# Four more projection units of the two layers as products of split operands, ahead of the gates

## What is computed

```
h    = rms_norm(x, attn_norm_g)
proj = h @ w_in                       # 1024 x 4768, float32
c_q, c_kv, k_rope, gq, gk, gv, pool_in, gate_logits = split_columns(proj, IN_SIZES)
o_mla, o_gqa, o_pool = mla_branch(...), gqa_branch(gq, gk, gv), pool_branch(pool_in)
gates  = sigmoid(gate_logits)         # 3 x 1024 columns
merged = sum over branches of gates[b] * (o_b @ w_branch_b)
x = x + merged @ w_out
x = x + (silu(u_gate) * u_val) @ w_down,   u = conv(rms_norm(x) @ w_up)
```

## Time and profile before

| what | us |
|---|---|
| median of 3 runs | 2156.4 (2155.51 to 2159.56) |
| the profiled execution | 2156.41 |
| its span, first to last instruction | 2154.6 |
| outside the span | 1.8 |
| TensorE busy in the span | 2047.8 (95%) |
| VectorE busy | 893.4 (41%) |
| ScalarE busy | 628.6 (29%) |
| layer 0: from 1220 us on; layer 1: from 1687 us on | about 467 each |

### The profile page before, as it was taken

How to read it: one execution, slowest core, us unless ns; L and a number is a source line. 1 busy time by engine, 2 the same in 40 slices (tenths; PEclk the granted TensorE clock), 3 DMA queues, 4 the chain that set the end, 5 groups by cost and what they waited for, 6 DMA issues and landing times.

```text
span 2154.6 us, 31774 instructions
## 1 busy us (share of the span) xinstructions
PE 2047.8 (95%) x12318; PEld 1314.1 (61%) x12319; DVE 893.4 (41%) x1608; ACT 628.6 (29%) x967; POOL 31.1 (1%) x45
## 2 busy tenths in 40 slices
PE   6998999999999999999999999999999999999999
PEld 4863333333333333333333598879999888789999
DVE  2522221112212221122122346866885348766874
ACT  1422111111111111111111225443654144634553
POOL 0000000000000000000000020000000020000000
PEclk9998999999999999999999999999999999999999
DMA  9786999399999999999499564413654554334563
GB/s 345 268 328 265 393 417 402 134 417 417 417 419 418 417 417 418 419 418 417 179 371 417 217 195 128 147 55 103 203 189 158 140 158 132 111 99 145 171 204 108
DMA packets 222040, 580.36 MB, mean 269 GB/s; under 512 B 23520, under 2 KB 142048, under 8 KB 185984
## 3 DMA queue, kind: packets, MB, share of 16 engines
q1 hardware_dynamic: 221952, 579.09, 70.7%
HBM read 577.74 MB, written 1.31 MB: 269 GB/s over the span
## 4 chain that ended last, share of the span: by engine, by line
PE 69%; DMA 11%; SPq 8%; DVE 6%; ACT 3%; issue 3%; ACTq 0%; DVEq 0%
PE bank L1080 13%; DMA ring<-in_w_gu 9%; PE bank L1136 8%; PE bank L807 6%; SPq L680 4%; SPq L682 4%; PE bank L1424 3%; PE bank L1425 3%; PE bank L1426 3%; PE bank L1032 3%; PE bank L1046 3%; PE bank L1211 2%; PE bank L877 2%; PE bank L1213 2%; PE bank L1212 2%
## 5 line engine op out<-in xcount | busy, mean ns | idle before, releaser
L1080 PE MATMUL bank<-ring,heap 128*64 128x512 f32 x2176 | 494.6, 603 | 30.4 <-DMA ring<-in_w_gu 30.4
L1080 PEld LDWEIGHTS bank<-ring,heap 128*64 128x64 f32 x2176 | 149.0, 138 | 359.2 <-issue 266.0
L2045 DVE TENSOR_SCALAR heap<-bank 128x256 f32<-128x256 f32 (+1 forms) x72 | 26.7, 412 | 725.2 <-PE bank L1080 696.5
L1136 PE MATMUL bank<-ring,heap 128*64 128x512 f32 (+1 forms) x1152 | 255.1, 595 | 0.0
L1424 PE MATMUL bank<-h_hi,w_hi 128*128 128x256 f32 x640 | 181.7, 284 | 3.4 <-DVE w_lo L2321 3.4
L2321 DVE TENSOR_TENSOR w_lo<-ring,w_hi 128x2048 fp32r<-128x2048 f32 (+1 forms) x64 | 142.4, 2226 | 97.6 <-ACT w_hi L1739 97.6
L1425 PE MATMUL bank<-h_lo,w_hi 128*128 128x256 f32 x640 | 181.1, 283 | 0.0
L1426 PE MATMUL bank<-h_hi,w_lo 128*128 128x256 f32 x640 | 181.1, 283 | 0.0
L1575 ACT ACT_TABLE_LOAD x32 | 41.1, 1283 | 471.8 <-DVE heap L2045 470.2
L1136 PEld LDWEIGHTS bank<-ring,heap 128*64 128x64 f32 (+1 forms) x1152 | 78.7, 135 | 150.7 <-issue 145.0
L1739 ACT ACTIVATE w_hi<-ring 128x2048 fp32r<-128x2048 f32 (+1 forms) x64 | 119.1, 1860 | 145.4 <-PE bank L1426 85.9
(11 more groups left out here) (336 smaller groups left out, 3065.3 us busy)
## 6 DMA issues: line engine op xcount, KB each, us to landing
ring<-in_w_gu SPq DMA_DIRECT2D x256, 1024.0 KB, 19.1
ring<-in_w_down SPq DMA_DIRECT2D x128, 1024.0 KB, 21.4
ring<-in_ffn_w_up SPq DMA_DIRECT2D x44, 1024.0 KB, 7.7
ring<-in_w_in SPq DMA_DIRECT2D x32, 1024.0 KB, 5.6
ring<-in_w_ada SPq DMA_DIRECT2D x24, 1024.0 KB, 10.8
ring<-in_ffn_w_down SPq DMA_DIRECT2D x16, 1024.0 KB, 6.7
ring<-in_w_out SPq DMA_DIRECT2D x8, 1024.0 KB, 4.9
ring<-in_w_in SPq DMA_DIRECT2D x3, 2048.0 KB, 27.1
```

Of the source, the lines that this page charges most:

```text
L1080: last = mm(psum[g][both[f], :], xgT[:, k % 4, k // 4, :], wt[:, g, :, :, f, :].rearrange("p i c n -> p (i c) n"), start=False, stop=k == ...
L1136: last = mm(psum[2][FEW * f:FEW * f + n, :], hidT[:, o:o + n], wt[:, 512 * f:512 * (f + 1)], start=k == 0, stop=k == DT - 1)
```

## The change

In each layer four of the plain units become split units: `gq1`, `po0`, `gk`, `po1`. `cq`, `ckv`, the key part, `gq0` and `gv` stay plain.

- The order on PE after `ckv`: `gq0` plain, `gq1` split, `po0` split, `gv` plain, `gk` split, `po1` split, then the small sums and the gates as before. `gq1` and `gk` are now products of `h`, so DVE only copies them out of PSUM.
- The list of pieces has `w_po0` ahead of `w_gkv`. With that `w_po0` is early; `w_po1` waits for `gq0` and `ckv`, `ga0` for the split of `w_gq1`, `ga1` for that of `w_po0`, and the later pieces lie one place further in the ring.
- ACT makes `w_hi` of `gq1` and `po0` right after its first root of the layer, ahead of `var1`; DVE makes the two `w_lo` ahead of its work on `ss1`.
- `h_hi` and `h_lo` are made in halves, right after `h`; the scaling of `xT` comes behind them. The first split unit waits for the first half, and at k = 4 for the second.
- `w_hi` of `gk` is made by ACT behind `gq1`, of `po1` behind `po0`, of `ga0` behind `gk`, of `ga1` behind `po1`; DVE follows each.

```diff
-NG, NB, NW = 12, 6, 22
+NI, NG, NB, NW = 4, 16, 6, 26
+FIRST = ("w_gq1", "w_po0", "w_gkv", "w_po1")
...
-        layer = [("w_lat", 8 * 416), ("w_gq0", 8 * 256), ("w_gq1", 8 * 256), ("w_gkv", 8 * 384), ("w_po0", 8 * 256),
+        layer = [("w_lat", 8 * 416), ("w_gq0", 8 * 256), ("w_gq1", 8 * 256), ("w_po0", 8 * 256),
+                 ("w_gkv", 8 * 384), ("w_po1", 8 * 256), ("ga0", 8 * 256), ...
...
+                        if first and k % 4 == 0:
+                            done("h1", 2 + k // 4)
...
+                def by_unit(name, n):
+                    done("wlo", n + 1)
+                    b = halves(lay(name))
+                    for a in range(2):
+                        last = split_tile(b[:, a, :], early_unit(n)[2:], P * a, (h_hi, h_lo), DT, n == 0 and a == 0)
+                    last.then_inc(lay_full.sem, 1)
...
-                for i in range(2):
-                    arrived(f"w_gq{i}")
-                    tiles(f"gq{i}", piece(lay_stream, f"w_gq{i}", 8), 0, raw)
+                arrived("w_gq0")
+                tiles("gq0", piece(lay_stream, "w_gq0", 8), 0, raw)
+                by_unit("gq1", 0)
+                by_unit("po0", 1)
                 arrived("w_gkv")
-                tiles("gk", w, 0, raw)
                 ... gv ...
-                for i in range(2):
-                    arrived(f"w_po{i}")
-                    tiles(f"po{i}", piece(lay_stream, f"w_po{i}", 8), 0, h)
+                by_unit("gk", 2)
+                by_unit("po1", 3)
...                                                     (ACT)
                 f(L["rs"][:, 1, :], c2, ACT.Sqrt).then_inc(S["std1"].sem, 1)
+                lead(0)
+                lead(1)
                 ready("var1")
...
-                f(h_hi[:, :, :], L["h"], ACT.Copy).then_inc(S["hhi"].sem, 1)
+                for i in range(2):
+                    f(h_hi[:, 4 * i:4 * i + 4, :], L["h"][:, 4 * i:4 * i + 4, :], ACT.Copy).then_inc(S["hhi"].sem, 1)
+                full("gq1")
+                lead(2)
+                out_of("po0", L["pool"][:, 0:2, PAD:PAD + T])
+                lead(3)
+                out_of("gv", L["gv"], lambda b: two(b)[:, :, 0:P])
+                full("gk")
+                lead(4)
                 out_dve("gk")
...
-                out_of("gv", L["gv"], lambda b: two(b)[:, :, 0:P])
-                lead(0)
-                out_of("po0", L["pool"][:, 0:2, PAD:PAD + T])
                 out_of("po1", L["pool"][:, 2:4, PAD:PAD + T])
-                lead(1)
+                lead(5)
...                                                     (DVE)
                 ready("vecs")
+                rest_early(0)
+                rest_early(1)
                 r1 = L["rs"][:, 0, :]
...
+                ready("h1")
+                for i in range(2):
+                    ready("hhi", i + 1)
+                    v.tensor_tensor(h_lo[:, 4 * i:4 * i + 4, :], ...).then_inc(S["h1"].sem, 1)
                 c.mark(v.tensor_tensor(xT[:, :, :], xT[:, :, :], ...))
                 taken(by_token(L["gq"][:, 0:2, :], two(full("gq0"))))
-                taken(by_token(L["gq"][:, 2:4, :], two(full("gq1"))))
-                taken(by_token(L["gk"], two(full("gk"))))
+                taken(v.tensor_copy(L["gq"][:, 2:4, :], two(full("gq1"))))
+                rest_early(2)
+                rest_early(3)
+                taken(v.tensor_copy(L["gk"], two(full("gk"))))
                 own("gk")
                 c.settle()
-                ready("hhi", 1)
-                v.tensor_tensor(h_lo[:, :, :], ...).then_inc(S["h1"].sem, 1)
-                rest_early(0)
+                rest_early(4)
                 b = two(full("sslat"))
```

More of the change, by code:

```diff
@@ L324, in build @@
         exp_stream = Stream(EXPERT, RING)
-        layer = [("w_lat", 8 * 416), ("w_gq0", 8 * 256), ("w_gq1", 8 * 256), ("w_gkv", 8 * 384), ("w_po0", 8 * 256),
-                 ("w_po1", 8 * 256), ("ga0", 8 * 256), ("ga1", 8 * 256), ("w_uq", 2 * 768), ("w_ukv", 1024), ("ga2", 8 * 256),
-                 ("pool_w", 4 * P)] + [(f"ga{n}", 8 * 256) for n in range(3, NG)] \
+        layer = [("w_lat", 8 * 416), ("w_gq0", 8 * 256), ("w_gq1", 8 * 256), ("w_po0", 8 * 256),
+                 ("w_gkv", 8 * 384), ("w_po1", 8 * 256), ("ga0", 8 * 256), ("ga1", 8 * 256), ("w_uq", 2 * 768), ("w_ukv", 1024), ("ga2", 8 * 256),
+                 ("pool_w", 4 * P)] + [(f"ga{n}", 8 * 256) for n in range(3, NG - NI)] \
             + [(f"br{b}{h}", 4 * 512) for h in range(2) for b in range(3)] + [(f"wo{i}", 8 * 256) for i in range(4)] \
@@ L332, in build @@
         lay_stream = Stream(layer, LRING, again=True)
-        LAY_LAST = {"w_lat": "ckv", "w_gq0": "gq0", "w_gq1": "gq1", "w_gkv": "gv", "w_po0": "po0", "w_po1": "po1",
+        LAY_LAST = {"w_lat": "ckv", "w_gq0": "gq0", "w_gkv": "gk",
                     "w_uq": "uq3", "w_ukv": "uv1", "pool_w": "pl1", "up0": "up1"}
@@ L502, in build @@
         heads = [f"m{h}" for h in range(NH)] + [f"g{h}" for h in range(NH)]
-        order = [("ss1", "dve"), ("cq", "dve"), ("ckv", "dve"), ("gq0", "dve"), ("gq1", "dve"), ("gk", "dve"),
-                 ("gv", "act"), ("po0", "act"), ("po1", "act"), ("sslat", "dve"), ("ssgq", "dve"),
+        order = [("ss1", "dve"), ("cq", "dve"), ("ckv", "dve"), ("gq0", "dve"), ("gq1", "dve"), ("po0", "act"),
+                 ("gv", "act"), ("gk", "dve"), ("po1", "act"), ("sslat", "dve"), ("ssgq", "dve"),
                  ("ssgk", "dve"), ("ga0", "act"), ("ga1", "act")]
@@ L534, in build @@
         S = {name: signal(f"l_{name}", per) for name, per in {
-            "vecs": 1, "sq1": 4, "var1": 1, "std1": 2, "xg": 2 * DT, "h1": 6, "lsq": 1, "lvar": 1, "lstd": 1, "lat": 1,
+            "vecs": 1, "sq1": 4, "var1": 1, "std1": 2, "xg": 2 * DT, "h1": 7, "lsq": 1, "lvar": 1, "lstd": 1, "lat": 1,
             "gsq": 1, "gvar": 1, "gstd": 1, "gn": 1, "rope_g": 1, "qvar": 1, "qstd": 1,
@@ L565, in early_unit @@
         def early_unit(n):
-            name, rows = (f"ga{n}", DT) if n < NG else (f"br{(n - NG) % 3}{(n - NG) // 3}", 4) if n < NG + NB else \
+            name, rows = (FIRST[n], DT) if n < NI else (f"ga{n - NI}", DT) if n < NG else (f"br{(n - NG) % 3}{(n - NG) // 3}", 4) if n < NG + NB else \
                 (f"wo{n - NG - NB}", DT)
             hi, lo = (x[:, n % 2, :].rearrange("p (a b) -> p a b", a=rows) for x in (w_hi, w_lo))
-            return name, piece(lay_stream, name, rows), hi, lo
+            return name, piece(lay_stream, name, rows)[:, :, 0:hi.shape[2]], hi, lo
         def used(name):
@@ L580, in used @@
             if name.startswith("ga"):
-                return S["wlo"], int(name[2:]) + 1
+                return S["wlo"], NI + int(name[2:]) + 1
+            if name in FIRST and name not in LAY_LAST:
+                return S["wlo"], FIRST.index(name) + 1
             if name.startswith("br"):
@@ L1202, in drained_act, with split_tile @@
                     pe.wait_ge(lay_drained["act"].sem, lay_drained["act"].at(LF.drain[LF.index[name]][1], l))
-                h = lambda k: L["h"][:, k, :]
-                def split_tile(out, w, cols, x, nk):
+                def split_tile(out, w, cols, x, nk, first=False):
                     hi, lo = w
                     for k in range(nk):
+                        if first and k % 4 == 0:
+                            done("h1", 2 + k // 4)
                         wh, wl = hi[:, k, cols:cols + P], lo[:, k, cols:cols + P]
@@ L1214, in split_tile @@
                     return last
-                def gates(n):
[L1218 to L1222, removed]
+                def by_unit(name, n):
[4 more added lines that the diff above has]
+                    last.then_inc(lay_full.sem, 1)
+                def gates(n):
+                    by_unit(f"ga{n}", NI + n)
                 raw = lambda k: xgain[:, k, :]
@@ L1381, in _ @@
                         if i == 0 and k % 2 == 0:
-                            done("h1", 2 + k // 2 + 1)
+                            done("h1", 3 + k // 2 + 1)
                         for a in range(2):
@@ L2129, in _, with rest_early @@
                     .then_inc(S["vecs"].sem, 1)
+                def rest_early(n):
+                    _, src, hi, lo = early_unit(n)
+                    ready("whi", n + 1)
+                    v.tensor_tensor(lo, src, hi.bitcast(F32), ALU.subtract).then_inc(S["wlo"].sem, 1)
                 ready("vecs")
+                rest_early(0)
+                rest_early(1)
                 r1 = L["rs"][:, 0, :]
```

36 lines of the change are left out of this document (16 added, 20 removed).

## The result

The changed kernel takes 2143.55 us in the median of 4 runs (2143.3 to 2146.3), the kernel before in the same job 2155.95 us (2155.22 to 2159.56). The ratio is 0.9944, 95% interval [0.9929, 0.9958]. Forecast were 2147.2 us (2142.8 to 2151.5), a ratio of 0.9957. In a second job (the experiment e5_again) it was 2144.95 against 2156.11, 0.9946 [0.9932, 0.9960]. The profiled execution took 2143.49 us with a span of 2141.6, 13.0 less than before.

The account below looks back on a forecast made before the run. PE alone was taken to set the pace in the changed stretch. Four units of 1.15 us in each of two layers, with preparation hidden, give 9.2 us: 2156.4 - 9.2 = 2147.2 us, range 2142.8 to 2151.5.

Parts of the forecast that it names:

- The price of a unit: PE's gate products: a split unit takes 5.76 us against 6.91 plain, a gain of 1.15 us each.
- Cover in layer 0: Layer 0: DVE's ss1 starts 2.1 us late, but the 4.29 us idle ahead of ckv absorbs it.
- Layer 1, the narrow place: Layer 1: w_po0 lands at about 1696.2, making ss1 4.0 us late; the 4.29 us ahead of ckv just suffices.
- Rival 1: Layer 1: w_po0 lands late; at 1705.9 it costs 8.2 us, giving 2155.4; chance 0.06, shared with several small waits.
- Rival 2: Some of the eight preparations on ACT or DVE come 1 to 2 us late, halving the gain: 2150 to 2152; chance 0.11.
- Rival 3: Split products follow at 0.107 us, gaining 14 us: 2142; chance 0.08, shared with all clock stretches gone.
- Rival 4: PE loses or finds a half-clock stretch, 1.7 us each: 2144 to 2149; forecast with this scatter 0.72.
- The sum: Whole kernel: 2156.4 us less 9.2 us for two layers of four units gives 2147.2 us.

Follow-up runs that it names:

- e5_again: The changed kernel with nothing edited, measured a second time: 2144.95 us against 2156.11 for the kernel before, ratio 0.9946.
- the clean pair: e6_sums_only and e7_sums_and_products, compared for the change itself: layer 0 takes 461.30 and 456.70 us.
- e4_cover: The changed kernel with two extra thrown-away DVE subtractions of 2.29 us per layer ahead of the first w_lo: 2150.34 us, ratio 0.9973.
- e10_before_again: The kernel before with nothing edited, profiled a second time: the layers take 932.01 us.
- e8_two_products: The changed kernel without the product of w_hi and h_lo in gq1, po0, gk and po1: 2129.02 us, ratio 0.9887.
- e3_ssq: The changed kernel with the ssq sums issued in two groups, each ahead of one half of ga2: 2139.08 us, ratio 0.9919.
- e6_sums_only: The kernel before with only the ssq sums split into two groups, each ahead of one half of ga2: 2149.77 us, ratio 0.9971.
- e7_sums_and_products: The changed kernel with the ssq sums in two groups between the halves of ga2, run again: 2139.79 us, ratio 0.9926.
- e9_narrow_weights: The changed kernel with 96 extra products on 64-column weights ahead of each half of po0: 2167.78 us, the kernel before 2160.82.

## Why the prediction was right

- **The price of a unit (1.15 us): right.** 4.60 us in layer 0, in the first profile and in the clean pair, and 4.60 in layer 1; 2.20 for two units; 7.68 for four times sixteen instructions fewer. The distance of 0.120 us, read from `ga0` and `ga1`, held for units that follow one another in the new place. The counts are the forecast ones, L1214 x640 for x512 and L810 x192 for x448 in the groups that multiply `h` or the stream from the ring.
- **Cover in layer 0: right.** Forecast: `ss1` 2.1 us late, cover of 4.29 + 1.2. Measured: 1.9 late, 2.40 us left ahead of `ckv`. e4_cover, which takes the cover away, put 1.1 us on the path where its expectation gives 1.3.
- **Layer 1, the narrow place: no time lost, but with luck.** `w_po0` was forecast 9.3 us after the layer's start and came at 9.2; `ss1` was forecast 4.0 us later and was 3.85. But the prediction took its place before from one profile, in which `w_lat` landed late. Against e10_before_again, with the same landing, `ss1` is 5.51 us late, the whole of the cover that the prediction counted (4.29 + 1.2). That it just sufficed (4.60 us of gain) was not foreseen; by the prediction 1.5 us were to be left.
- **Rival 1 (late `w_po0`) did not happen**; e4_cover shows what lateness costs there, a wait of 3.54 us and a half-clock stretch behind it, which the prediction's price of 1 us for each us leaves out. Its price for a landing at 1711 is also added up wrong (13.3 us, not 13.5). A `w_po0` that is itself late was not tried.
- **Rival 2 (partial cover) did not happen**: no idle time of PE in the changed stretch, and the preparation stays hidden at 3.84 us a unit.
- **Rival 3 (faster products): not at 128 columns of weights.** The distance stays 0.120; narrow weights reach 0.113.
- **Rival 4 (clock): the size of one stretch was right, the scatter was taken too small.** I gave the clock 2 to 3 us. The layers alone lost 4.9 to 8.3 us in unedited kernels, and the part ahead of layer 0, which the prediction left out, moved by 2.4 us between two profiles of one kernel (1218.79 and 1221.14) and by up to 6.3 between variants, though its code is the same in all. The clock there is a part of this: the three earliest starts (1216.3 to 1216.6) go with a granted clock of 0.986 ahead of layer 0, the others with 0.980 to 0.985. But it is not all: the first profiles before and after had 0.983 and 0.982.
- **The sum, and the chances.** The measured 2143.55 us lie inside the range, but not in its main part (2144.5 to 2149, a chance of 0.72). They lie in the part from 2142 to 2144.5, to which I gave 0.08 and for which I named faster products or the end of all half-clock stretches. Neither happened. The kernel got there by the 9.2 us and by 2 to 3 us that the sum has no term for. 9.2 of the 11.2 to 12.4 us by which the medians differ are the change's work. The other 2 to 3 us lie within the interval of the ratio. In the profiles the changed kernel and its variants begin layer 0 at 1216.3 to 1221.1 us, the kernel before and its variants at 1220.4 to 1222.6. Whether the change has a small part in that or it is chance stays open: too few profiles, and no mechanism shown.

## What to carry to other kernels

Where TensorE is busy without a break, a cheaper form of the same product is worth the difference in the distances of starts, times the count, provided each piece of its preparation is placed in a named gap; the gap that is nearly used up (here ahead of `ckv` in layer 1) is the one to measure. Before two profiles are subtracted, take out what each lost to the clock and to single landings: here one landing was worth 1.6 us, and the layers of a single profile lost 4.9 to 8.3 us to the clock, beside a gain of 9.2. And the clock is work to be had: putting full products between groups of one-column sums gave 0.3% of the median in the kernel before and 0.2% more on top of the change.

## What the hardware did that I had not expected

- Thirty-two products of one column in a row (3.63 us, busy without a break) were followed by a stretch at half clock in both layers of both kernels' profiles, and in every variant that keeps them in a row but for layer 0 of e8_two_products; two groups of 16 (1.84 us each) with 3.0 us of full products between them never were, in six layers. By the granted clock this is 1.2 GHz against 2.4. That PE shows as busy is no sign that the clock will stay.
- The stretches at the scores (at 1362 before, at 1813 after) disappeared along with those behind `ssq` (e3_ssq, e6_sums_only, e7_sums_and_products), though nothing was edited there; in the changed kernel's first profile there was one in layer 1 alone, in its second one in each layer. Over all profiles with the 32 sums in a row they stand in 11 of 18 layers, over those with two groups in 0 of 6, though the wait of about 1.5 us ahead of them is in all. How the one depends on the other stays open.
- A wait of 3.54 us cost 3.4 us again by the half-clock stretch behind it (e4_cover).
- The scatter of one kernel's runs goes with the mean granted clock: e3_ssq took 2133.01 and 2134.89 us at 0.992, and 2141.98 and 2142.11 at 0.988; 0.004 of 2134 us are 8.5.
- `w_lat` in layer 1, issued 8.1 us ahead of the layer in every profile, landed after either 6.6 to 6.9 or 8.4 to 8.9 us (7.0 in e9_narrow_weights), under both orders of the loads. The cause was not found.
